# First block's mixers: the order of one low part, three roundings and three modulation tiles around the forget gate's chain

## The reference, cut to what matters

```python
mod = cond @ ada_w[l] + ada_b[l]                     # nine vectors of 1024: shifts, scales, gates
hn = _modulate(_rms_norm(h, norm_g[l, 1]), sh2, sc2)
z = hn @ w_in[l]                                     # 256 x 2564: inputs of four mixers
o_a = _differential_attention(qa, ka, va, ...)       # two softmaxes, RMS-normed q and k
o_b = _conformer_conv(...)                           # causal depthwise conv, width 31
u, v = jnp.split(jax.nn.gelu(z_c), 2, axis=-1)       # gated unit: v = LN(v), mixed over 128 tokens
o_c = u * (W_s @ v + b)
log_f = jax.nn.log_sigmoid(z[..., FOX_F0:IN_COLS] + fox_fb[l])
o_d = _forgetting_attention(qd, kd, vd, log_f)       # logits + cumsum(log_f)
h = h + g2[:, None, :] * (concat(o_a, o_b, o_c, o_d) @ w_out[l])
```

## Time and profile before

| | |
|---|---|
| median of 3 runs | 2401.02 us (2400.06 to 2403.53) |
| the profiled execution: its time / its span | 2401.33 us / 2399.6 us |
| granted TensorE clock, mean over the span | 0.981 |
| busy share of the span: PE, PEld, DVE, ACT, POOL | 95%, 79%, 67%, 47%, 6% |
| chain that ended last: PE, DVE, ACT | 80%, 11%, 4% |
| DMA | 452.76 MB, mean 189 GB/s |
| mixers, layer 0 (262 to 402): PE busy, DVE busy, granted clock | 127.59 of 140 us, 101.53, 0.90 |
| mixers, layer 1 (842 to 980): PE busy, DVE busy, granted clock | 123.60 of 138 us, 100.92, 0.96 |

### The profile page before, as it was taken

How to read it: one execution, slowest core, us unless ns; L and a number is a source line. 1 busy time by engine, 2 the same in 40 slices (tenths; PEclk the granted TensorE clock), 3 DMA queues, 4 the chain that set the end, 5 groups by cost and what they waited for, 6 DMA issues and landing times.

```text
span 2399.6 us, 31812 instructions
## 1 busy us (share of the span) xinstructions
PE 2279.2 (95%) x11786; PEld 1906.7 (79%) x11796; DVE 1614.3 (67%) x1877; ACT 1124.9 (47%) x1307; POOL 134.5 (6%) x182
## 2 busy tenths in 40 slices
PE   5999899999999988999999989999999998999998
PEld 3787786788788787688878879988887887997887
DVE  5786884776677688555565668586566556867655
ACT  2434454434444455444444466554444446564443
POOL 1000033000000005100000000000000000000000
PEclk9999998999999999999999999999999999999999
DMA  8896653687588474265555554346555554434653
GB/s 289 290 318 206 194 176 96 209 282 248 165 296 284 153 233 140 93 210 183 184 193 182 185 141 141 123 158 201 183 175 193 192 185 138 139 119 158 193 192 105
DMA packets 321094, 452.76 MB, mean 189 GB/s; under 512 B 32392, under 2 KB 269802, under 8 KB 319978
## 3 DMA queue, kind: packets, MB, share of 16 engines
q1 hardware_dynamic: 317944, 440.96, 56.2%
q0 software_dynamic: 2784, 9.50, 1.2%
q10 hardware_dynamic: 274, 1.06, 0.1%
HBM read 450.43 MB, written 1.05 MB: 188 GB/s over the span
## 4 chain that ended last, share of the span: by engine, by line
PE 80%; DVE 11%; ACT 4%; issue 2%; POOL 2%; DMA 0%; POOLq 0%; DVEq 0%; ACTq 0%; SPq 0%
PE ps L551 19%; PE ps L553 19%; PE ps L552 19%; PE ps L544 4%; PE ps L545 4%; PE ps L546 4%; DVE wlo L1729 2%; PE ps L1019 2%; POOL side L2424 1%; PE ps L655 1%; PE ps L773 1%; PE ps L637 1%; PE ps L584 1%; PE ps L638 1%; PE ps L881 1%
## 5 line engine op out<-in xcount | busy, mean ns | idle before, releaser
L1729 DVE TENSOR_TENSOR wlo<-raw,whi 128x2048 fp32r<-128x2048 f32 (+1 forms) x348 | 791.5, 2278 | 399.6 <-ACT whi L1149 393.9
L1149 ACT ACTIVATE whi<-raw 128x2048 fp32r<-128x2048 f32 x346 | 660.1, 1910 | 282.7 <-PE ps L553 237.0
L551 PE MATMUL ps<-whi,xl 128*128 128x512 f32 x1472 | 593.7, 403 | 4.8 <-DVE u L1910 3.6
L553 PE MATMUL ps<-whi,xh 128*128 128x512 f32 x1472 | 575.1, 391 | 0.0
L552 PE MATMUL ps<-wlo,xh 128*128 128x512 f32 x1472 | 575.1, 391 | 0.0
L551 PEld LDWEIGHTS ps<-whi,xl 128*128 128x128 f32 x1472 | 277.2, 188 | 67.1 <-issue 4.8
L553 PEld LDWEIGHTS ps<-whi,xh 128*128 128x128 f32 x1472 | 277.1, 188 | 60.3
L552 PEld LDWEIGHTS ps<-wlo,xh 128*128 128x128 f32 x1472 | 277.5, 189 | 58.9 <-issue 4.8
L544 PE MATMUL ps<-xl,whi 128*128 128x256 f32 x864 | 253.7, 294 | 17.1 <-DVE wlo L1729 17.1
L551 PE MATMUL ps<-whi,hidl 128*128 128x512 f32 x640 | 252.2, 394 | 0.0
L553 PE MATMUL ps<-whi,hidh 128*128 128x512 f32 x640 | 249.2, 389 | 0.0
(11 more groups left out here) (372 smaller groups left out, 2578.3 us busy)
## 6 DMA issues: line engine op xcount, KB each, us to landing
raw<-in_ffn_w_in_dram SPq DMA_DIRECT2D x176, 512.0 KB
arena<-in_ada_w_dram SPq DMA_DIRECT2D x128, 512.0 KB, 5.7
raw<-in_w_in_dram SPq DMA_DIRECT2D x54, 1024.0 KB
raw<-in_ffn_w_out_dram SPq DMA_DIRECT2D x44, 1024.0 KB
raw<-in_w_ffn_gate_dram SPq DMA_DIRECT2D x88, 512.0 KB
raw<-in_w_ffn_up_dram SPq DMA_DIRECT2D x88, 512.0 KB
raw<-in_w_ffn_down_dram SPq DMA_DIRECT2D x44, 1024.0 KB
raw<-in_w_out_dram SPq DMA_DIRECT2D x16, 1024.0 KB
```

The lines of the kernel that those rows point to most:

```text
L551: pe.matmul(o, al, wh, start=start, stop=False, **kw)
L553: return pe.matmul(o, ah, wh, start=False, stop=stop, **kw)
L1149: act.activation(whi[:, k % 3, :], raw[:, k % 3, :], ACT.Copy).then_inc(hi_done, 1)
L1729: tt(a[0], a[1], a[2].bitcast(F32), ALU.subtract).then_inc(lo_done, 1)
```

## The change

On ACT the roundings of units 6 and 7, with the copy of unit 4 between them, move ahead of the forget gate's chain, so that with unit 5's three roundings stand there. On DVE tile 5 moves up beside tile 4, ahead of the gated unit's product; low part 5 and the forget bias move up into the layer norm, between its aggregate and its root; low part 6 stands right behind the norm; tiles 6 and 7 move behind the end of the forget gate, and low part 7 ahead of tiles 8 and 9. Nothing is added or taken out; PE's, SP's and POOL's lists are the same.

```diff
@@ ACT, mix0
                 hi(L, k0 + 5)
                 copy(3)
+                hi(L, k0 + 6)
+                copy(4)
+                hi(L, k0 + 7)
                 act.wait_ge(s["fx"], l + 1)
                 f, w = zt["f"][0:4, 0:S], zt["f"][0:4, S:2 * S]
                 st(act.activation(w, f, ACT.Abs))
                 st(act.activation(w, w, ACT.Exp, scale=-1.0))
                 act.activation(w, w, ACT.Ln, bias=ones_col[0:4, 0:1]).then_inc(s["fl"], 1)
 
-                hi(L, k0 + 6)
-                copy(4)
-                hi(L, k0 + 7)
                 copy(5)
@@ DVE, mix0
                 gelu_in(1, zt["gv"], zt["cg"])
-                tiles(4, 5)
+                tiles(4, 6)
                 dve.wait_ge(s["gu_e"], 2 * l + 1)
                 st(tt(zt["gv"], zt["gv"], zt["cg"], ALU.mult))
...
                 for b in range(2):
                     ins = dve.bn_aggr(lnmv[:, b, :], lnst[:, b, :])
                 st(ins)
+                lo(L, k0 + 5)
+                copied(L, zi["f"])
+                f, w = zt["f"][0:4, 0:S], zt["f"][0:4, S:2 * S]
+                ts(f, f, fb[0:4, l:l + 1], None, ALU.add).then_inc(s["fx"], 1)
                 mm, y, tmp, half = (lnr[:, i, :] for i in range(4))
...
                 tt(v, v, ngb[:, 1, l:l + 1, :].to_broadcast([P, 2, 256]), ALU.add).then_inc(s["gv"], 1)
-                tiles(5, 6)
-                lo(L, k0 + 5)
-
-                copied(L, zi["f"])
-                f, w = zt["f"][0:4, 0:S], zt["f"][0:4, S:2 * S]
-                ts(f, f, fb[0:4, l:l + 1], None, ALU.add).then_inc(s["fx"], 1)
-                tiles(6, 8)
+                lo(L, k0 + 6)
+
                 dve.wait_ge(s["fl"], l + 1)
...
                 ts(gcum[0:4, 1, :], gcum[0:4, 0, :], -1.0, None, ALU.mult).then_inc(s["foxcum"], 1)
-                lo(L, k0 + 6)
+                tiles(6, 8)
+                lo(L, k0 + 7)
                 tiles(8, 10)
-                lo(L, k0 + 7)
```

## The result

The changed kernel takes 2418.62 us (median of 5 runs, 2412.81 to 2420.0), the kernel before 2402.27 us beside it: a ratio of 1.0057, 95% interval 1.0041 to 1.0073.

What follows compares the result with a forecast made beforehand. PE, busy 95%, was taken as the bound, its chain meeting DVE's at the first differential scores; 2401.33 + 3.1 (layer 0) + 4.3 (layer 1) = 2408.7 us profiled, median 0.3 lower, 2408.4 us; range 2399.5 to 2417.

Steps and rivals of the forecast that it cites:

- the third rival: Rival, chance 0.20: unit 7 lands at 289.1, both tile trips 5.33 us; 2414.0 us, up to 2417 with unit 8's half clock.
- What bounds the stage: At the first differential scores PE's and DVE's chains arrive within 0.1 us; shortening PE's alone moves nothing behind.
- ACT's side: Forget gate's chain waits for unit 7's load, landing at 287.0; DVE's scans start at 292.8, 0.45 us sooner.
- the late bound: Latest landing of unit 7's load, 289.1, from the 8.0 us that unit 9's load took.
- The round trips: DVE waits for tiles 9 and 11: trips of 5.33 and 4.6 us; norm of q and k ends 3.1 us later.
- Behind the scores: PE's 6 to 7 us idle brings one half-clock stretch per layer: +3.1 us in layer 0, +4.3 in layer 1, norm's delay included.
- The sum: Whole kernel: 2401.33 + 3.1 + 4.3 = 2408.7 us for the profiled execution, median 2408.4 us.
- short round trips: Rival, chance 0.16: both tile trips take 3.89 us; +0.9 us a layer, 1.2 for layer 1's clock: 2404.0 us.
- not slower: Rival, chance 0.12: tiles never hold DVE up, trips below 3.4 us; norm 1.4 us sooner, 2398.3 or 2396.7 us.
- late and slow: The third rival, chance 0.20: unit 7's load lands late and tiles are slow; 2414.0 us, up to 2417.

Runs made afterwards that it cites:

- the late pair: Changed kernel with tiles 10 and 11 behind the norm of q and k instead of ahead of it; 2409.63 us, ratio 1.0042.
- the head alone: Kernel before with only tile 5 beside tile 4 and low part 5 and the forget bias inside the norm; 2404.08 us, ratio 1.0011.
- the zeros: Matmuls of zeros in PE's idle, results unchanged: on the head alone 2399.34 us; on the changed kernel 2414.64 us with 22, 2411.53 us with 19 and 30.
- the tail: DVE's low part 6 before the forget gate's end, tiles 6, 7 behind it, low part 7 before tiles 8, 9; changed kernel, ACT as before: 2412.87 us.
- the regrouped kernel without zeros: The head alone with DVE's tile pairs one step later from the norm of q and k on, no matmuls of zeros; 2395.08 us, ratio 0.9972.
- regrouped with zeros: The head alone, DVE's tile pairs one step later from the norm of q and k on, 12 zero matmuls ahead of the statistics; 2391.01 us, 0.9964.
- three kernels with zeros: Changed kernel with 22 zero matmuls (1.0057), changed kernel with 19 and 30 (1.0055), and regrouped with zeros (0.9964).

## Why the prediction was right, and where its size was off

The direction and the two chains were right, the size was not: +7.4 us forecast, about +14 measured. By the ratio the kernel stands at 2401.02 x 1.0057 = 2414.7 us, inside 2399.5 to 2417 but outside the forecast's own 2404 to 2413; the bare median, 2418.62, lies 1.6 us above the range. That the range held is owed to the third rival and not to the forecast's sum.

- **What bounds the stage**, two chains that meet at the first scores: right. PE won what was forecast (0.6 us of wait in place of 4.74, unit 5 in 5.9 us), and nothing of it reached the scores. The statistics came 2.0 us later than forecast and at half clock, which the prediction had allowed for; PE was early for the scores all the same.
- **ACT's side**: the load of unit 7 was taken to land at 287.0, and landed at 286.98 + 2.1 = 289.1 on before's line, the late bound. "Here DMA has nothing else" was the wrong reason: two tiles go out just ahead of this load (277.33 to 279.05), as ahead of unit 9's, whose 8.0 us I set aside. With one tile just ahead, in the kernel with ACT's part alone, it landed in 6.2 us. That is 2.1 us a layer.
- **The round trips**: the mechanism is shown by the late pair. Sizes: end of tile 7 to start of 9 was 5.99 us (297.14 to 303.13) where 5.33 stood. The second trip ended not on tile 11 but on tile 10, issued at 300.88 and landed at 307.31, 6.4 us later, behind unit 8's load. I had written that the queue was nearly drained for tile 11 and had not asked when tile 10 lands. Tile 11 starts at 308.70, 4.3 us behind the end of tile 9, where 4.6 stood. The two slips (+0.7 and -0.3 us) nearly cancel: 308.7 + 2.1 = 310.8 is 2.5 us over the 308.3 of the sum, 2.1 of it from unit 7. Norm and scores: +5.5 us a layer, +3.1 forecast.
- **Behind the scores**: the term that failed most. I charged one half-clock stretch of 3.2 us, as behind the idle of 4.74 us, +0 and +1.2 us. It held for 13.6 us in each, 11.3 and 9.0 of them over the scores and unit 8, +3.6 and +3.8 us. That the loss behind the scores is clock is shown for the head alone, by the zeros. For the changed kernel they show it in layer 0 (14.2 down to 9.3 us); in layer 1 most of it stayed, and why is open. No row of before had an idle in front of scores; an upper bound by the scores and unit 8 wholly at half clock was to be had.
- **The sum**: 2 x 5.5 + 3.6 + 3.8 = 18.4 us to the second scores of both layers, of 18.0 between the two profiled executions. Around them the two executions differ as well (-2.1 us ahead of layer 0's gelu, -2.6 us between layer 0's second scores and layer 1's gelu, +4.2 us behind layer 1's second scores), and these I can't assign, though half-clock stretches come and go there too: so the close fit of 18.4 to 18.0 is in part luck. By the ratio of all runs the loss is about 14 us, not 18.
- **Rivals**: short round trips and not slower are out; "late and slow" was the true case for ACT and the first trip, and its 2414.0 to 2417 the better number.
- **ACT's share** is under-told in the prediction, which speaks of the tail as the cause. With the head in place, the tail costs 3.8 and 4.8 us of the norm's end and ACT's order 3.6 and 1.8, each alone; together 6.1 and 6.0.

## What to carry to other kernels

Where two chains meet at one point without slack, ask of every edit which of them it lengthens: work moved out from under a wait, here two tiles, takes with it every transfer that its buffer releases, and in a queue with a written order all loads behind. A rounding moved ahead of a chain brings its load's landing into that chain. Idle of PE can be charged twice, once as idle and again as half clock in the work that follows, and that for longer than the idle was: read the clock in every stretch behind it, and do not carry its price from one place to another.

## What the runs showed of the hardware

- The half clock behind an idle is not a fixed price. Behind 4.74 us it held 3.4 us; around the waits of 5.38 and 6.57 us, with scores of 32 rows following, it held 13.6 us in each layer. Behind 2.81 us it came in the head alone (statistics in 3.36 us) and not in the regrouped kernel without zeros (1.98 us).
- Idle is not all that goes ahead of it: it came with no idle noted ahead of the first scores (regrouped with zeros, layer 1), where 12.1 us passed between the scores in place of the 9.1 at full clock.
- Matmuls of zeros in the idle kept the clock at 1.00 in layer 0 of the head alone (308 to 322), and did not keep the half clock away in layer 1 of three kernels with zeros (12.1, 12.1 and 12.1 us between the scores).
- A tile of 512 KB is not landed 3 us after its issue once a load of 1 MB is in flight: 6.4 us for tile 10 (300.88 to 307.31), 7.6 with zeros on PE (302.75 to 310.37). The estimate of 3.2 us from the Trainium skill's page "DMA: Bandwidth & Descriptors", section on the anatomy of one DMA, is worked out from a fit for transfers on GpSimd's path, and these are SP's; it is below all that these rows show. The nearest of them is 3.7 us for tile 8 of the changed kernel, issued at 295.84 with the queue idle and used on landing at 299.50.
- A load of 1 MB lands 6.2 us after its issue with one tile just ahead of it (285.56 to 291.73), 7.8 and 8.0 with two (279.15 to 286.98, and unit 9's before). In the changed kernel unit 8's load, with two tiles ahead, took 8.3 us (297.67 to 305.94), though DMA had carried nothing from 287 to 295.
